# Longer assumed delays between engines in the list scheduler of a hybrid decoder layer

## The reference

```
z = rmsnorm(h) @ w_in                       # 6144 columns: q, f, i, og | ga, gb
fgate = lb + (1 - lb) * sigmoid(f);  k = 1 - fgate          # group A: 8 heads of 128 x 128
S_t = diag(f_t) S_{t-1} + k_t v_t^T ;  o_t = S_t^T q_t      # chunks of 64 tokens
o_a = headnorm(o) * silu(og)
u = ga * sigmoid(gb);  c = depthwise_conv31(u)              # group B
o_b = silu(groupnorm(c))
h = h + concat(o_a, o_b) @ w_out
h = h + (silu(hf @ w_gate) * (hf @ w_up)) @ w_down          # hf = rmsnorm(h), 5632 hidden
y = rmsnorm(h)
```

## Time and profile before

| | us |
|---|---|
| median of 3 runs | 1734.06 (1733.07 to 1734.46) |
| profiled execution, its own time | 1737.78 |
| its span, slowest core (core 0) | 1736.2 |
| spans of the eight cores | 1724.9 to 1736.2 |
| PE busy, share of the span | 1655.8, 95% |
| DVE and ACT busy | 523.1 and 518.4, 30% each |

### The profile page before, as it was taken

How to read it: one execution, slowest core, us unless ns; L and a number is a source line. 1 busy time by engine, 2 the same in 40 slices (tenths; PEclk the granted TensorE clock), 3 DMA queues, 4 the chain that set the end, 5 groups by cost and what they waited for, 6 DMA issues and landing times.

```text
span 1736.2 us, 31827 instructions; the slowest of 8 cores (1724.9 to 1736.2 us)
## 1 busy us (share of the span) xinstructions
PE 1655.8 (95%) x13252; PEld 1165.2 (67%) x13252; DVE 523.1 (30%) x949; ACT 518.4 (30%) x979; POOL 151.2 (9%) x112
## 2 busy tenths in 40 slices
PE   3789999999899999999999999999999999999998
PEld 3566677676566554446666666666666688888887
DVE  3226836476754444442111111111111101010106
ACT  3355636576655666111010001000100010110102
POOL 1010111111312000001010010101010000000000
PEclk9799999999999999999999999999999999999999
DMA  9659555758669966339573738465564365666665
GB/s 204 167 112 174 94 73 77 142 91 146 131 135 183 243 137 119 134 127 158 74 98 49 98 51 140 65 82 76 72 85 62 49 115 93 92 92 92 92 117 206
DMA packets 266795, 197.22 MB, mean 114 GB/s; under 512 B 3707, under 2 KB 254971, under 8 KB 262319
## 3 DMA queue, kind: packets, MB, share of 16 engines
q0 software_dynamic: 210304, 111.15, 49.6%
q1 hardware_dynamic: 39421, 74.60, 13.7%
q10 hardware_dynamic: 16928, 9.44, 2.0%
HBM read 271.57 MB, written 28.04 MB: 173 GB/s over the span
## 4 chain that ended last, share of the span: by engine, by line
PE 87%; DMA 4%; DVE 3%; ACT 3%; issue 2%; DVEq 0%; POOL 0%; ACTq 0%; SPq 0%; POOLq 0%
PE PS L668 50%; PE PS L1362 18%; PE PS L1217 6%; DMA arena<-w_in 3%; PE PS L588 3%; PE PS L527 3%; PE PS L751 2%; PE PS L1038 1%; PE PS L470 1%; DMA arena<-xall 1%; PE PS L1384 1%; DMA scn<-arena 0%; PE PS L912 0%; DVE arena L691 0%; DVE arena L921 0%
## 5 line engine op out<-in xcount | busy, mean ns | idle before, releaser
L668 PE MATMUL PS<-arena 128*128 128x344 bf16 (+4 forms) x6144 | 923.7, 311 | 0.9 <-ACT arena L990 0.5
L668 PEld LDWEIGHTS PS<-arena 128*128 128x128 bf16 x6144 | 596.9, 98 | 306.9 <-issue 4.0
L1362 PE MATMUL PS<-arena 128*128 128x256 bf16 x2816 | 310.4, 273 | 0.0
L1362 PEld LDWEIGHTS PS<-arena 128*128 128x128 bf16 x2816 | 274.8, 98 | 34.5 <-issue 1.7
L1318 DVE TENSOR_TENSOR arena<-PS,arena 128x352 bf16<-128x352 f32 (+1 forms) x132 | 68.5, 519 | 544.5 <-PE PS L668 543.9
L1316 ACT ACTIVATE arena<-PS 128x352 f32<-128x352 f32 (+1 forms) x132 | 60.7, 459 | 554.4 <-PE PS L668 554.4
L1217 PE MATMUL PS<-arena 128*128 128x512 bf16 x512 | 113.1, 379 | 2.0 <-ACT arena L1063 1.7
L1371 ACT ACTIVATE arena<-arena 128x256 bf16<-128x256 f32 x64 | 26.7, 417 | 274.5 <-DVE arena L1369 274.4
L1369 DVE TENSOR_TENSOR arena<-PS,arena 128x256 f32<-128x256 f32 x64 | 27.1, 424 | 253.9 <-PE PS L1362 240.9
L1217 PEld LDWEIGHTS PS<-arena 128*128 128x128 bf16 x512 | 49.6, 98 | 60.8 <-issue 3.4
L347 POOL DMA_DIRECT2D arena<-w_gate x22 | 25.1, 1142 | 690.8 <-PE PS L668 492.8
(11 more groups left out here) (167 smaller groups left out, 1101.1 us busy)
## 6 DMA issues: line engine op xcount, KB each, us to landing
arena<-w_in POOLq DMA_DIRECT2D x32, 1024.0 KB, 12.6
arena<-xall SPq DMA_DIRECT2D x24, 1024.0 KB, 8.3
arena<-w_gate POOLq DMA_DIRECT2D x22, 1024.0 KB, 9.5
arena<-w_up POOLq DMA_DIRECT2D x22, 1024.0 KB, 12.3
arena<-w_down POOLq DMA_DIRECT2D x8, 2816.0 KB, 22.4
arena<-arena SPq DMA_DIRECT2D x32, 263.0 KB, 7.1
arena<-sh SPq DMA_DIRECT2D x16, 512.0 KB, 4.8
shn<-arena ACTq DMA_DIRECT2D x16, 512.0 KB, 4.7
```

Source lines behind the costliest of these rows:

```text
L668: ins = e.matmul(ps(b)[:, 0:n], wv[:, k, m * 128:(m + 1) * 128], src3[:, k, c0:c0 + n], start=(k == 0), stop=(k == 15))
L1362: ins = e.matmul(ps(b)[:, 0:256], hm3[:, k, ti * 128:ti * 128 + 128], wv[:, k, :], start=(k == 0), stop=(k == NFF - 1))
```

## The change

One line of `Prog.schedule`: the delays that the model adds between an operation's end and a dependent operation on another engine. Those of operations on ACT, DVE and POOL grow from 0.3 to 0.7 us, that of PE's from 0.45 to 0.6 us.

```diff
     def schedule(self):
-        lat = {"pe": 0.45, "act": 0.3, "dve": 0.3, "pool": 0.3, "sp": 0.1}
+        lat = {"pe": 0.6, "act": 0.7, "dve": 0.7, "pool": 0.7, "sp": 0.1}
         for o in self.ops:
```

## The result

The changed kernel takes **1749.41 us** (median of five executions; four lie between 1746.56 and 1750.82, the fifth took 1822.79), the kernel before 1734.06: ratio **1.0082** (the fifth left out), 95% interval 1.0065 to 1.0100. It is slower by 0.8%, where the prediction said +0.2% and ended its range at 1745. The sign was right and the size was not.

A forecast was written before the change was run, and what follows sets the result against it. PE was taken as the bound from the FFN on, with order mattering only at its holes in recurrences and convolution. Terms summed to +3.8 us on a core without core 0's accident; forecast 1737 us, range 1728 to 1745.

The forecast's parts named there:

- Part 1: Start of the recurrences: eight transpose matmuls that filled a wait for weights now run behind it, +0.7 us.
- Part 2: Recurrences: more bulk work between chain steps removes PE waits, -5.5 us, and a half-clock loss, -1.2 us.
- Part 3: From the last L864 into the convolution, bulk groups run short: +6.4 us idle, +2.0 copy wait, +1.7 clock.
- the walk: New order followed from L864's end to the first L1038: 14.0 us with 6.5 of work, idle 7.5 for 1.1.
- The wait for the copies: Fifth block of L1038 waits longer for shifted copies, as less PE work stands beside them: +2.0 us, bounds -1 and +4.
- the clock there: Handover and copy wait: some 12 us idle of 27 lowers PE's clock, +1.7 us, bounds 0 to 4.
- my three terms: Last L864 to fifth block of L1038: handover idle +6.4, wait for copies +2.0, lower clock +1.7 us.
- Part 4: Convolution's end, twelfth block to the L1217 needing the last group: -1.5 us, plus 1.2 for clock, -0.3 together.
- The base: Slowest core: without core 0's accident core 2 at 1734.1 us is slowest, so the profiled time rises by only 1.7.
- (b): Rival: queues make the waits, recurrences give nothing (-2), handover and end cost their upper values; 1746 us, chance 0.19.
- (a): Rival: margin works as meant, all 10.3 us of core 3's recurrence waits go; 1724 us, chance 0.19.
- (c): Rival: nothing comes of it, the same idle time in other places; 1734 us, chance 0.10.

The follow-up runs named there:

- `g_handover`: Kernel before, old delays, with five bulk matmul groups forced ahead of the last L864: ratio 1.0090, +13.6 us per core against before.
- `e_fill`: Changed kernel in its own order, plus useless matmuls where PE waits: ratio 1.0060, +10.1 us per core against the kernel before.
- `e_quarter_after`: Changed kernel with the shifted copies of groups 2 to 7 cut to a quarter of their bytes: +14.5 us per core against the kernel before.
- `e_others_only`: Changed kernel with the delay behind PE back at 0.45 us, 0.7 behind ACT, DVE and POOL: +14.6 us per core against the kernel before.
- `e_conv_only`: Old delays up to the convolution's recording, new ones for the last recurrence, convolution and output projection: +12.3 us per core against the kernel before.
- `e_pe_only`: Changed kernel with the delays behind ACT, DVE and POOL back at 0.3 us, 0.6 behind PE: ratio 1.0050, +0.5 us per core against before.
- `e_short`: Shorter delays than the kernel before, 0.3 us behind PE and 0.15 behind the others: ratio 1.0059, +4.2 us per core against before.
- `f_tail_late`: Kernel before with one instruction moved, the last L1055 put behind six groups of L1217: ratio 1.0037, +6.1 us per core against before.
- `f_after_again`: The changed kernel run once more, unaltered, beside other kernels: ratio 1.0097, +15.3 us per core against the kernel before.
- `f_pe_early`: Kernel before with the delay behind PE 0.6 for 0.45 us, only for what is recorded ahead of the convolution: ratio 0.9975, -2.8 us per core.
- `g_early_54`: Kernel before with delays 0.5 us behind PE, 0.4 behind ACT, DVE and POOL, only ahead of the convolution: ratio 0.9994, -1.0 us per core.

## Why the prediction was right or wrong

**What bounds the kernel: right.** The stretch of the FFN is the same to the hundredth (613.00 us); all that changed lies in the stages named.

**Part 1, the start: not to be told.** The first L588 started at 123.9 and 127.6 us in two executions of the same kernel; 0.7 us drowns in it.

**Part 2, the recurrences: right in kind, a little too small.** -5.5 and -1.2 for the clock were forecast. The stage gave back 7.7 us in both; of core 3's waits 7.4 us went, L784's wholly and L817's from 3.0 to 1.1 us (I had said that it would be gone), and no half clock is left. What I had not seen is that 4.5 of it is to be had without any stock.

**Part 3, the handover: the walk was right, its neighbours were not.** The four waits were forecast at 1.9, 2.7, 0.9 and 1.9 us and are 1.88, 2.53, 0.89 and 2.01 on core 0, and the same in `g_handover`; PE's idle time came to 7.3 us where the walk had 7.5. The failed steps are the two terms behind it. The wait for the copies grew by 4.2 on core 0 (6.18 for 2.01; over the cores it is 5.0 to 7.4 us where it was 1.2 to 3.4), where I had put 2.0 with 4 as the bound: I kept the 12.8 us from the first to the fifth block, but the first block now runs at half clock, so the copies are issued later, and the distance became 14.9; 1.4 us of that is the block itself, the rest the copies. By my own figures, 9.9 us of work and then 7.0 in an unchanged 12.8, the term was also +2.9 and not +2.0. And the clock there was +1.7 in the sum. From the last L864 to the fifth block the changed kernel took 31.0 and 32.6 us with 12 us less work, where it took 30.2: +12.8 to +14.4, against the 10.1 of my three terms.

**The middle of the convolution: missing from the sum.** I took the twelve blocks' stretch as unchanged. It costs 3.8 us: half clock in the block behind the copy wait (3.60 us for 1.91 on core 0; over the cores 3.56 where it was 2.59, for four of them ran it slowly before too), a wait of 1.60 us of L668 for L990, and some 1 us of work that moved in. `g_handover`, with the old delays, has 0.9 of it, so the rest comes from the new interleaving, which I had not walked.

**Part 4, the end: wrong, -0.3 for +6.** The 5.7 us to the fourteenth block came true (5.5), and so did the one wait of some 5 us for L1063 (5.82). Failed: the 27.4 us from there, which are 32.5 on seven cores (34.6 on core 0). I had walked along PE and taken what stands between the last L1055 and L1217 as the limit. But that chain starts late: the last L1055 comes 31.8 us after the twelfth block's end where it came 27.1 on core 3, because it waits for L1053. I had counted more changes of ACT's table there (nine for six) and given them no term; the trace has ten loads for six in S5, 5.1 us of ACT's time. That ACT is the limit is argued, not separated by a run: S5 is 38.0 us on nearly every core of the changed kernel, `e_fill`, `e_quarter_after`, `e_others_only` and `e_conv_only`, which all have ten loads, whatever PE's clock and its copy waits are, and about 34 us in the kernels with six; `e_pe_only` and `e_short` have ten and 38 us too, but `f_tail_late` has eight and 38.5, by its own late L1055. I also had the second wait for a copy (2.0 to 3.0 us over the cores) nowhere; in the kernel before the same block waits for its diagonal (L1018, 1.3 to 2.4 us). `e_quarter_after` shows that it is worth little by itself, for the diagonal and L1057 are next late. The two waits of L1055 and L1217 are together 7.1 us; then come 1.9 us of clock in S6 in place of 1.2.

**The base: wrong in principle.** I let the slowest core be an accident of core 0, whose removal would halve the rise. In 59 executions of the kernel before with all cores at whole clock, each of the eight cores was the slowest at least 4 times and at most 12; the slowest lies 5.2 us (scatter 1.8) over the mean of the cores. Such accidents are dealt out anew in every execution. The time is the mean plus some 5 us, and a change of the mean goes into it whole: +3.8 by my own terms should have stood against 1734.06, not 1.7.

**The sum.** One part from an experiment and three from the stages close it: `g_handover` +13.6, the end (S5 and S6) +6.1, the middle +3, the recurrences -7.7 make +15.0, where `f_after_again` has +15.3. That `f_tail_late` is at +6.1 too is chance: it gets its number by a late L1055, the changed kernel by a late chain. Of the rivals (b) came nearest, 1746, with half of its mechanism: the handover and the end do cost more than the recurrences give, but it had the recurrences give nothing, which was wrong, and it took 0.5 us for an end whose own bound was +4. (a) and (c) are out.

**Still open.** Why a given order inside the recurrences leaves 408 or 412 us is not settled; the slack counted in the order doesn't tell `f_pe_early` from `g_early_54`, and neither does the number of ACT's table loads in S1 (43 and 47, before 45). The last group's lateness in the changed kernel is shown by its waits and goes with ACT's four added loads; a run with the changed order on PE and ACT's halves back in pairs was not made, nor was it separated which move ahead unpairs them.

## What to carry to other kernels

Work that needs nothing is a stock: before spending it earlier, look where its last pieces stand, and walk that place instruction by instruction, because a hole there can bring lower clock (here some 5 us) and a later DMA issue with it. Look at the order on every engine, not only at that of the busiest: at the end of the convolution it is ACT's that changed for the worse. A global number in a scheduler is worth splitting by stage: here a longer delay behind PE alone, up to the convolution, is worth -0.25%, and longer delays everywhere +0.8%. And judge the time of a many-core program from the mean of the cores, not from the accident of the slowest.

## What the hardware showed that I had not expected

- Half clock after holes that are not long: four waits of 1.9, 2.5, 0.9 and 2.0 us with 4 us of work in between put the next block at 3.29 us for 1.91. The length of a single wait doesn't settle it: ahead of the fifteenth block a wait of 1.99 us was followed by half clock on core 5 (3.58) and not on core 3 (1.91), one of 2.99 us was on core 0 (3.60) and one of 2.73 us was not on core 6 (1.91). Filling such holes with useless matmuls gained 5 us.
- A copy within SBUF of a quarter of the bytes lands only 1.5 us sooner (6.9 for 8.4 us), and eight issues hold SyncE for about 8 us either way.
- The place of one matmul (`f_tail_late`) is worth 6 us of 1734; by the stages 4.3 of waiting and 2.5 of clock behind it.
